# Three changes of order in a two-layer, two-block transformer kernel: third latent tile's weights, norm of x, first chunks of the next ada sums

## The chip, the cores and the metric

The kernel runs on one core of one Trainium2 chip. The metric is the device time of one execution in microseconds, as the median of several runs. The engines are TensorE (PE, matrix products), VectorE (DVE), ScalarE (ACT), GpSimd (POOL) and the queue of SyncE (SP), which issues most of the transfers. Each runs its own instructions in the order in which they are written, and they wait for each other by semaphores.

## The reference

Two transformer blocks of two layers each work on the same x of 256 tokens by 1024 columns, in float32. The first block modulates x by sums made from a conditioning vector c (six rows "ada" of 1024 for each layer), and normalises after each residual. The second takes the x of the first, projects it by a w_in of 4128 columns and runs three kinds of attention, of which one has latents at the end of these columns. Cut to what matters here:

```python
c_act = silu(c)
for l in range(2):                                    # first block
    ada = c_act @ w_ada[l] + b_ada[l]                 # sh1, sc1, gt1, sh2, sc2, gt2
    u = x * (1.0 + sc1) + sh1
    y = mixer(u, ...w_in[l]...)                       # attention, convolution, gates
    x = layer_norm(ALPHA * x + (1.0 + gt1) * y, ln_mix_g[l], ln_mix_b[l])
    u = x * (1.0 + sc2) + sh2
    h = square(relu(u @ w_up[l])) @ w_down[l]         # w_up 1024 x 4096
    x = layer_norm(ALPHA * x + (1.0 + gt2) * h, ln_ffn_g[l], ln_ffn_b[l])
for l in range(2):                                    # second block
    h = rmsnorm(x, ln_mix_g[l])
    proj = h @ w_in[l]                                # 1024 x 4128
    ...                                               # three attentions, gates, w_o, gated FFN
return rmsnorm(x, final_norm_g)
```

## The kernel before, in words

**Weights.** Every matrix of weights streams through a ring of four slots (class Weights, L91 to L190). A group is two chunks of 128 rows: 128 partitions by 2 x 512 numbers (2 x 344 for w_in of the second block, where a group comes as two transfers). SP asks for a group once the slot's last low part is made (L117 to L121); ACT makes the high part, a rounded copy (L128), after the landing and after PE has used the slot's last group; DVE makes the low part, raw less high (L134); PE multiplies three times for each chunk and each of the two token tiles: high by high, low by high, high by low (L148 to L150). Four groups make a tile of 512 (or 344) columns, 48 matmuls. So all engines go through the same list of groups, each in its own hand-written order of work between them.

**The first block's FFN.** Up-tile f is followed by down-tile f - 1 in the list of groups; T_FF is 8. DVE makes for each step f four low parts of down-tile f - 1, then in `hidden` (L1077) the squares of h, four low parts of up-tile f + 1, a row of the sum for gate 2 (`gate2_chunk`), chunk updates of the next layer's first ada sums (`next_chunk`, L1062: two instructions on 1024 columns, rows of w_ada times a number of c_act added to `ada_first`), and the low parts of the turned h (`aT`). In step 0 these are chunks 0 and 1, in step f chunk f + 1. SP issues the two fills of a chunk (`next_first`) ahead of the requests for an up-tile; they wait until the chunk two before is used.

**The start of layer 1.** DVE adds the last residuals, makes the rows of u for both token tiles with low parts of the first tile's weights between, then norms x itself for both token tiles (`normed`, two instructions of 1024 columns for each), which releases POOL's four loads for the convolution. After these come the low parts of the next weights, in a loop of four tiles, each with a row of the sum for gate 1 (L880) behind it.

**The start of the second block.** Four tiles of w_in, the latent columns, come first, into different banks of PSUM; the first is scaled by x_rstd on ACT (`take_scaled`) when it leaves its bank, and the fourth needs that bank. x_rstd is the root that POOL makes (`x_root`) from squares that ACT makes of the normed x (`square_x`). The norm of x (`last_x`) stands on DVE between the low parts of the second tile. At its end `first_left` is raised. POOL waits for that, issues a gather of 1.5 MB for the bias tables, and then makes the roots. SP too waits for it, having asked for two tiles of weights; it issues ten small loads of tables, then asks for the third tile.

## Time and profile before

| | us |
|---|---|
| median of 3 runs | 1920.86 (1920.22 to 1922.59) |
| the profiled execution | 1923.12 |
| its span in the profile | 1921.2 |
| PE busy, share of the span | 1807.1, 94% |
| DVE busy | 1310.8, 68% |
| ACT busy | 871.5, 45% |
| mean granted TensorE clock | 0.979 |

Times in the rows are microseconds from the span's start. In a timeline a row has the start, the duration, the engine, the line of the kernel, the operation, the tile it writes and those it reads, and the shapes; xN stands for N instructions merged into one row. A number in brackets is the idle time of the engine just before, with what ended it. Matmuls overlap, so their pace is read from their starts and not from their durations. SPq is SyncE's queue.

### The profile page before, as it was taken

How to read it: one execution, taken by the hardware profiler on the slowest of the kernel's cores; microseconds unless marked ns; L12 is line 12 of the kernel's file. 1: busy time of each engine (PE TensorE's matmuls, PEld its weight loads, DVE VectorE, ACT ScalarE, POOL GpSimd, SP SyncE). 2: the span in 40 equal slices, each digit the busy share in tenths (PEclk: the TensorE clock that was granted, in tenths of full speed). 3: DMA queues.
4: the chain of work that ended last, by engine and by line, in shares of the span. 5: the costliest groups of instructions: out<-in, count | busy, mean ns of one | idle time of the engine just before them, and what ended most of it. 6: DMA issues, size and time to landing. Idle time of an engine off the chain costs nothing.

```text
span 1921.2 us, 26005 instructions
## 1 busy us (share of the span) xinstructions
PE 1807.1 (94%) x8358; PEld 1423.2 (74%) x8358; DVE 1310.8 (68%) x2025; ACT 871.5 (45%) x1460; POOL 53.0 (3%) x112
## 2 busy tenths in 40 slices
PE   7989999998989999999699999999999999999998
PEld 3755777886765678887698777788879976778886
DVE  4679887667778986557455788655555478875555
ACT  1434434443434334443355565444445466644443
POOL 0000000000000000000000000000000000000000
PEclk9999999999999999998899999999999999999999
DMA  8755567773755547663456433465556653345554
GB/s 294 251 158 171 178 206 249 244 249 118 258 165 176 171 166 236 204 200 112 158 164 225 131 121 121 154 195 174 179 165 186 207 162 122 103 154 186 185 173 134
DMA packets 211186, 345.94 MB, mean 180 GB/s; under 512 B 20153, under 2 KB 95847, under 8 KB 210837
## 3 DMA queue, kind: packets, MB, share of 16 engines
q1 hardware_dynamic: 208774, 337.27, 54.4%
q0 software_dynamic: 2032, 6.97, 1.1%
q8 instruction: 53, 0.87, 0.2%
q10 hardware_dynamic: 288, 0.52, 0.1%
q14 instruction: 39, 0.32, 0.1%
HBM read 343.62 MB, written 1.07 MB: 179 GB/s over the span
## 4 chain that ended last, share of the span: by engine, by line
issue 52%; PE 30%; DVE 10%; DVEq 4%; ACT 1%; POOLq 1%; DMA 1%; SPq 1%; POOL 0%; ACTq 0%
PE prod L148 5%; PE prod L150 5%; PE prod L149 5%; PE acc L148 4%; PE acc L150 4%; PE acc L149 4%; DVE w_lo L134 3%; DVE conv_acc L917 2%; DVEq L916 2%; PE acc L1244 2%; PE turn L213 1%; DMA ada_rest<-in_w_ada_dram 1%; DVEq L775 1%; DVE stats L765 0%; DVE x_res L1013 0%
## 5 line engine op out<-in xcount | busy, mean ns | idle before, releaser
L134 DVE TENSOR_TENSOR w_lo<-w_raw,w_hi 128x1024 fp32r<-128x1024 f32 (+3 forms) x568 | 642.1, 1150 | 339.1 <-ACT w_hi L128 334.5
L128 ACT CAST w_hi<-w_raw 128x1024 fp32r<-128x1024 f32 (+3 forms) x568 | 554.2, 990 | 416.4 <-PE acc L150 197.0
L148 PE MATMUL prod<-w_hi,hT_hi 128*128 128x512 f32 (+1 forms) x880 | 332.2, 378 | 8.2 <-ACT kv_up L1687 1.8
L150 PE MATMUL prod<-w_hi,hT_lo 128*128 128x512 f32 (+1 forms) x880 | 323.9, 368 | 0.0
L149 PE MATMUL prod<-w_lo,hT_hi 128*128 128x512 f32 (+1 forms) x880 | 322.8, 367 | 0.0
L148 PE MATMUL prod<-w_hi,uT_hi 128*128 128x512 f32 x592 | 244.7, 413 | 17.1 <-DVE w_lo L134 8.0
L150 PE MATMUL prod<-w_hi,uT_lo 128*128 128x512 f32 x592 | 237.9, 402 | 0.0
L149 PE MATMUL prod<-w_lo,uT_hi 128*128 128x512 f32 x592 | 237.7, 402 | 0.0
L148 PEld LDWEIGHTS prod<-w_hi,hT_hi 128*128 128x128 f32 x880 | 166.4, 189 | 39.9 <-issue 7.3
L150 PEld LDWEIGHTS prod<-w_hi,hT_lo 128*128 128x128 f32 x880 | 166.6, 189 | 24.0
L149 PEld LDWEIGHTS prod<-w_lo,hT_hi 128*128 128x128 f32 x880 | 167.1, 190 | 21.2
L148 PEld LDWEIGHTS prod<-w_hi,uT_hi 128*128 128x128 f32 x592 | 113.4, 192 | 56.2 <-issue 17.4
L150 PEld LDWEIGHTS prod<-w_hi,uT_lo 128*128 128x128 f32 x592 | 113.6, 192 | 27.8
L149 PEld LDWEIGHTS prod<-w_lo,uT_hi 128*128 128x128 f32 x592 | 113.8, 192 | 24.5
L148 PE MATMUL acc<-w_hi,aT_hi 128*128 128x512 f32 x272 | 109.6, 403 | 7.3 <-DVE w_lo L134 4.5
L917 DVE SCALAR_TENSOR_TENSOR conv_acc<-hpad,conv_wT,conv_acc 128x256 f32<-128x256 f32 x232 | 102.5, 481 | 10.5 <-issue 1.3
L150 PE MATMUL acc<-w_hi,aT_lo 128*128 128x512 f32 x272 | 108.8, 400 | 0.0
L149 PE MATMUL acc<-w_lo,aT_hi 128*128 128x512 f32 x272 | 108.7, 400 | 0.0
L148 PE MATMUL acc<-w_hi,hT_hi 128*128 128x512 f32 (+1 forms) x144 | 57.2, 397 | 19.8 <-DVE w_lo L134 17.7
L148 PEld LDWEIGHTS acc<-w_hi,aT_hi 128*128 128x128 f32 x272 | 51.9, 191 | 22.0 <-issue 5.2
L1244 PE MATMUL acc<-ada_raw,c_wide 128*128 128x512 f32 x128 | 62.2, 632 | 0.0
L149 PEld LDWEIGHTS acc<-w_lo,aT_hi 128*128 128x128 f32 x272 | 51.9, 191 | 12.7 <-issue 0.2
(318 smaller groups left out, 2396.1 us busy)
## 6 DMA issues: line engine op xcount, KB each, us to landing
w_raw<-in_w_in_dram SPq DMA_DIRECT2D x72, 512.0 KB, 4.4
w_raw<-in_w_in_dram SPq DMA_DIRECT2D x192, 172.0 KB, 2.3
w_raw<-in_w_up_dram SPq DMA_DIRECT2D x64, 512.0 KB, 4.7
w_raw<-in_w_down_dram SPq DMA_DIRECT2D x64, 512.0 KB, 4.5
ada_raw<-in_w_ada_dram SPq DMA_DIRECT2D x52, 512.0 KB, 6.7
w_raw<-in_w_gate_dram SPq DMA_DIRECT2D x96, 256.0 KB, 3.2
w_raw<-in_w_ffn_gate_dram SPq DMA_DIRECT2D x88, 256.0 KB, 3.4
w_raw<-in_w_ffn_up_dram SPq DMA_DIRECT2D x88, 256.0 KB, 4.2
```

The costliest lines, as they stand in the source:

```text
L128: act.copy(self.hi[:, s, 0:cols], self.raw[:, s, 0:cols]).then_inc(self.hi_done, 1)
L134: dve.tensor_tensor(self.lo[:, s, 0:cols], self.raw[:, s, 0:cols], self.hi[:, s, 0:cols].bitcast(F32), ALU.subtract).then_inc(self.lo_done, 1)
L148: pe.matmul(out, a_hi, w_hi, start=first and c == 0, stop=False)
L149: pe.matmul(out, a_hi, w_lo, start=False, stop=False)
L150: mm = pe.matmul(out, a_lo, w_hi, start=False, stop=last and c == chunks - 1)
L213: t = pe.transpose(self.bank[b][0:rows, cols], src, self.ident)
L775: dve.drain()
L916: dve.drain()
L917: dve.scalar_tensor_tensor(out, rows, w, out, ALU.mult, ALU.add)
L1244: mm = pe.matmul(acc[0][:, :], c_wide[:, 2 * i + k, :], ada_raw[:, i, k * NT:(k + 1) * NT], start=i + k == 0, stop=False)
```

## The change

Three places are reordered.

- In layer 0's FFN, chunks 0 and 1 of the next layer's ada sums leave `hidden` of step 0. In step 1, chunk 0 stands behind the first two low parts of down-tile 0 and chunk 1 behind the other two. A drain follows chunk 1 too.
- At the start of layer 1, the norm of x of each token tile stands behind the first and the second low part of the loop, not ahead of all.
- At the start of the second block, SP asks for the third latent tile (groups 8 to 11) ahead of its wait for `first_left` and of the table loads. On DVE three low parts (6, 7, 8) stand between the norms of the two token tiles instead of two, and 9 to 11 behind `first_left`; on ACT the high parts 8 to 11 stand around the squares of x instead of behind them.

```diff
@@ first block, DVE, start of a layer
                     take_u_lo(3)
-                    for tok in range(TOKS):
-                        dve.drain()
-                        normed(x_res[:, tok, :], x_res[:, tok, :], tok, ln_vec[:, 0, :], ln_vec[:, 1, :]).then_inc(x_ready, 1)
...
                     for i in range(4):
                         W.split_lo(dve, Pos(4 + i, (l, G1), (t, 4)))
 
+                        if l > 0 and t == 0 and i < TOKS:
+                            dve.drain()
+                            normed(x_res[:, i, :], x_res[:, i, :], i, ln_vec[:, 0, :], ln_vec[:, 1, :]).then_inc(x_ready, 1)
@@ first block, DVE, next_chunk and hidden
                     if k == DC - 1:
                         dve.drain().then_inc(next_done, 1)
-                    elif k == 0:
+                    elif k < 2:
                         dve.drain()
...
                     if l < LAYERS - 1:
-                        for k in ((0, 1) if f == 0 else (f + 1,) if f < T_FF - 1 else ()):
-                            next_chunk(k)
+                        if 0 < f < T_FF - 1:
+                            next_chunk(f + 1)
...
                 for f in range(1, T_FF):
-                    split(Pos(at, (l, G1), (f, 8)))
+                    for g in range(0, 4, 2):
+                        split(Pos(at + g, (l, G1), (f, 8)), 2)
+                        if f == 1 and l < LAYERS - 1:
+                            next_chunk(g // 2)
@@ second block, SP
-                for t in range(2):
+                for t in range(3):
                     in_tile(IN2_T - LAT_TILES + t, layer(l, 4 * t, G2))
                 if l == 0:
                     sp.wait_ge(first_left, 1)
...
-                with sp.Fori(2, LAT_TILES) as t:
-                    in_tile(t + (IN2_T - LAT_TILES), Pos(0, (l, G2), (t, 4)))
+                for t in range(3, LAT_TILES):
+                    in_tile(IN2_T - LAT_TILES + t, layer(l, 4 * t, G2))
@@ second block, ACT
-                for tok in range(TOKS):
-                    square_x(2 * l, tok)
                 if l == 0:
-                    split(layer(l, 8, G2), 4, KG * IN2_W)
+                    split(layer(l, 8, G2), 1, KG * IN2_W)
+                    square_x(2 * l, 0)
+                    split(layer(l, 9, G2), 2, KG * IN2_W)
+                    square_x(2 * l, 1)
+                    split(layer(l, 11, G2), 1, KG * IN2_W)
+                else:
+                    for tok in range(TOKS):
+                        square_x(2 * l, tok)
@@ second block, DVE
-                    for tok in range(TOKS):
-                        split(layer(l, 4 + 2 * tok, G2), 2, KG * IN2_W)
-                        last_x(tok).then_inc(x_halves, 2)
+                    split(layer(l, 4, G2), 2, KG * IN2_W)
+                    last_x(0).then_inc(x_halves, 2)
+                    split(layer(l, 6, G2), 3, KG * IN2_W)
+                    last_x(1).then_inc(x_halves, 2)
                     dve.drain().then_inc(first_left, 1)
+                    split(layer(l, 9, G2), 3, KG * IN2_W)
...
-                with dve.Fori(1 if l == 0 else 0, LAT_TILES) as t:
+                with dve.Fori(2 if l == 0 else 0, LAT_TILES) as t:
                     split(Pos(4, (l, G2), (t, 4)), 4, KG * IN2_W)
```

## Rows read from the trace of the kernel before

**Rows 1.** Busy time by stretch: stretch, length, busy us, granted clock, DMA share, GB/s.

```profile
920.00:940.00 20.00, 5.46 (x35) 5.18 (x33) 4.44 (x6) 3.65 (x10) 3.61 (x11) 0.73 0.55 186
```

**Rows 2.** Waits of PE, whole span: who for whom, us in total, times, longest.

```profile
PE acc L148 <- DVE w_lo L134: 22.2, 6, 15.2
```

**Rows 3.** Timeline of DVE, layer 0's FFN, between steps 0 and 1.

```profile
291.48 5.05 DVE L1070 SCALAR_TENSOR_TENSOR ada_first<-ada_raw,c_act,ada_first 128x1024 f32<-128x1024 f32 x4
296.45 1.28 DVE L241 SCALAR_TENSOR_TENSOR aT_lo<-turn,aT_hi 128x512 fp32r<-128x512 f32 x2
297.82 4.63 DVE L134 TENSOR_TENSOR w_lo<-w_raw,w_hi 128x1024 fp32r<-128x1024 f32 x4
```

**Rows 4.** Timeline of PE there: first matmul of down-tile 0, first of up-tile 2.

```profile
299.19 0.76 PE L148 MATMUL acc<-w_hi,aT_hi 128*128 128x512 f32 x1 [4.51 <-DVE w_lo L134]
...
312.96 0.39 PE L148 MATMUL prod<-w_hi,uT_hi 128*128 128x512 f32 x1
```

**Rows 5.** Busy time behind that hole: PE, PEld, DVE, ACT, POOL, then granted clock.

```profile
299.20:304.40 5.20, 5.20 (x12) 4.09 (x13) 4.46 (x5) 0.00 (x0) 0.00 (x0) 0.50 0.78 246
```

**Rows 6.** Timeline of ACT there: the four high parts of down-tile 0.

```profile
289.63 2.00 ACT L128 CAST w_hi<-w_raw 128x1024 fp32r<-128x1024 f32 x2
...
295.21 1.04 ACT L128 CAST w_hi<-w_raw 128x1024 fp32r<-128x1024 f32 x1
```

**Rows 7.** DMA issues of the page: count, KB each, median us from issue to landing.

```profile
w_raw<-in_w_up_dram SPq DMA_DIRECT2D x64, 512.0 KB, 4.7
```

**Rows 8.** Timeline of DVE at the start of layer 1, norm of x and after.

```profile
489.66 1.28 DVE L774 SCALAR_TENSOR_TENSOR x_res<-x_res,mv,ln_vec 128x1024 f32<-128x1024 f32 x1
...
494.96 1.22 DVE L134 TENSOR_TENSOR w_lo<-w_raw,w_hi 128x1024 fp32r<-128x1024 f32 x1
496.27 0.75 DVE L880 SCALAR_TENSOR_TENSOR proj<-ada_raw,c_act,ada_b 128x512 f32<-128x512 f32 x1
```

**Rows 9.** Timeline of PE there: first matmuls of the second and the third tile.

```profile
496.23 0.80 PE L148 MATMUL prod<-w_hi,uT_hi 128*128 128x512 f32 x1 [3.54 <-DVE w_lo L134]
...
509.97 0.49 PE L148 MATMUL prod<-w_hi,uT_hi 128*128 128x512 f32 x1 [0.92 <-ACT proj L626]
```

**Rows 10.** Timeline of ACT there: high part of the third tile's third group.

```profile
508.29 1.05 ACT L128 CAST w_hi<-w_raw 128x1024 fp32r<-128x1024 f32 x1 [0.98 <-DMA w_raw<-in_w_in_dram]
```

**Rows 11.** Timeline of SP's queue: the request for that group.

```profile
500.12 0.37 SPq L121 DMA_DIRECT2D w_raw<-in_w_in_dram  x1
```

**Rows 12.** Timeline of SP's queue, second block: requests for weights from the third tile on.

```profile
930.37 29.12 SPq L121 DMA_DIRECT2D w_raw<-in_w_in_dram  x30
```

**Rows 13.** Timeline of ACT there: third tile's high parts, then the first tile's banks emptied.

```profile
938.93 1.62 ACT L128 CAST w_hi<-w_raw 128x688 fp32r<-128x688 f32 x2 [13.22 <-DMA w_raw<-in_w_in_dram]
...
942.23 0.98 ACT L1693 ACTIVATE proj_b<-prod,x_rstd 128x344 f32<-128x344 f32 x2
```

**Rows 14.** Timeline of POOL there: first operation behind the gather, last of the roots.

```profile
935.56 0.19 POOL L1644 TENSOR_TENSOR x_squares<-x_squares,small 128x1 f32<-128x1 f32 x1 [9.56 <-issue]
...
938.40 0.19 POOL L1658 TENSOR_TENSOR x_rstd<-x_rstd 128x1 f32<-128x1 f32 x1
```

**Rows 15.** Timeline of DVE there: low parts of the second tile, around the first norm.

```profile
915.63 1.66 DVE L134 TENSOR_TENSOR w_lo<-w_raw,w_hi 128x688 fp32r<-128x688 f32 x2
...
919.95 1.66 DVE L134 TENSOR_TENSOR w_lo<-w_raw,w_hi 128x688 fp32r<-128x688 f32 x2
```

**Rows 16.** Timeline of PE there: third tile, fourth tile, and what follows it.

```profile
940.66 0.65 PE L148 MATMUL acc<-w_hi,hT_hi 128*128 128x344 f32 x1 [15.20 <-DVE w_lo L134]
...
950.87 0.32 PE L148 MATMUL prod<-w_hi,hT_hi 128*128 128x344 f32 x1
...
958.44 3.61 PE L2286 MATMUL acc<-gates,proj_b 128*128 128x256 f32 x16
```

**Rows 17.** Timeline of POOL: power beside weight low parts (480.46), and with DVE idle.

```profile
480.46 1.34 POOL L591 TENSOR_TENSOR rstd<-var_eps,small 128x1 f32<-128x1 f32 x1
...
937.57 0.55 POOL L1646 TENSOR_TENSOR x_rstd<-x_squares,small 128x1 f32<-128x1 f32 x1
```

## Prediction, made before the changed kernel was run

> **What bounds the kernel now.** I read the table of 20 us stretches over the whole span first. PE is busy 94% of the time and most stretches of the feed-forward parts show it at 20.00 of 20. So only the holes can be bought, and I looked for the holes beside the three edited places. The deepest of the whole run is one of them: PE is busy 5.46 of 20 us at 920 to 940 [rows 1]. Next, what PE waited for: the low parts of weights, for the accumulating products 22.2 us in six waits, the longest 15.2 [rows 2]. Last, the timelines of every engine around each hole. They show three holes, all ended by a low part on DVE: 4.51 us before 299.19 [rows 4], 3.54 before 496.23 [rows 9], 15.20 before 940.66 [rows 16]. Each has a second price: PE comes back at the lower clock. Right behind the first hole the granted clock is 0.50 (1.2 GHz) and 12 matmuls fill 5.20 us [rows 5]. The reader should see in each timeline what DVE, or the queue, did just before the low part that PE missed; that is what the change moves.
>
> **Part 1, layer 0's FFN.** PE ends up-tile 1 at 294.68 (299.19 less 4.51) [rows 4]. DVE then still has the sum row of gate 2 to 291.5, four chunk updates of 1.26 us (291.48 to 296.5) and two aT low parts (to 297.7), and only at 297.82 the four low parts of down-tile 0 [rows 3]. The change takes the four chunk updates out. The aT low parts start at 291.5 and end at 292.8, then come weight low parts 1 and 2 at 1.16 each, done 294.1 and 295.3. Their high parts are there at 291.6 [rows 6]. Chunk 0 (2 x 1.26) runs to 297.8, low parts 3 and 4 end at 299.0 and 300.2 (the last high part is there at 296.3 [rows 6]), chunk 1 to 302.7. The drain added behind chunk 1 costs about 0.1 us, by the gap of 0.1 between the aT parts and the weight parts [rows 3].
> PE wants group 1 at 294.7, and it is ready at 294.1. Before, the tile took from 299.19 to 312.96, 13.77 us, of which the first 12 matmuls took 5.2 at the lower clock and the other 36 took 8.5, 0.236 each [rows 4, 5]. All 48 at 0.236 are 11.3 us. A group is a quarter, 2.8 us, so groups 2 to 4 are wanted at 297.5, 300.3 and 303.2, all behind their low parts. The tile ends at 306.0: a gain of 7.0 (4.5 of hole, 2.5 of clock).
> What is late next: up-tile 2. On SP its four requests stand behind the two fills of chunk 2, which wait for chunk 0. They go out at about 296.5 and 297.8, and the tile's first request at 298.3, still earlier than before. The median landing of such 512 KB is 4.7 us [rows 7], so 303.0; high part 1.05 and low part 1.2 [rows 6, 3] give 305.3, against 306.0 wanted. DVE is free for it at 304.1 (chunk 1 to 302.7, then two squares of h). The cover is 0.7 us; if two 512 KB fills ahead make it land after 8.1 us, the slowest such landing I use below, PE waits to 308.7 and the gain is 4.3. In step 1 DVE has three chunks: 8 low parts 9.6, six chunk updates 7.6, gate 2, squares and aT parts 1.3 each, 21.1 in all against a PE step of 22.7. Chunks 2 onward stand where they stood. I take 7.0, bounds 4.3 and 7.1.
>
> **Part 2, start of layer 1.** DVE spends 489.66 to 494.96 on the two norms of x, four instructions of 1.28 and drains [rows 8]; PE, free at 492.69, gets its low part at 496.2 [rows 9]. After: low part 1 from 489.9 to 491.1; norm of token tile 0 (2.65) to 493.8; an ada row of 0.75 [rows 8], to 494.6; low part 2 to 495.8; norm 1 to 498.5; row, 499.2; low part 3 to 500.4; row 501.2; low part 4 to 502.4. PE starts group 1 at 492.95 (ACT empties its bank), wants group 2 at 495.8 (ready at 495.9), group 3 at 498.7 (ready at 500.5: a new wait of 1.8), and ends the tile at 506.1. Before it ended at 509.05 (509.97 less 0.92 of waiting for ACT) [rows 9]. The next tile starts when ACT empties the bank, behind the high part at 508.29, whose weights were asked for at 500.12 and landed after 8.1 us [rows 10, 11]. That request now goes out at 500.5, 0.4 later, but the two ahead of it go out 5.0 and 2.4 earlier, into a DMA that was idle, so I let it land at about 505.7, an estimate between 4.7 us and 8.1 us after its request. PE restarts at 507.4 against 509.97: a gain of 2.5. Bounds: with 8.1 us again it restarts at 510.5, a loss of 0.6; with no new hole and no lower clock, 3.5 and 1.2 make 4.7. The lower clock after a hole of 1.8 us would cost at most what 6 matmuls at 0.43 cost over 0.236, 1.2. POOL's four loads behind the norm go out 3.5 us later; PE wants them 30 us on. That hides them.
>
> **Part 3, start of the second block.** The queue waits for the end of both norms, then issues ten table DMAs, and asks for tile 2's weights at 930.37 [rows 12]; ACT sees them at 938.93 [rows 13]. Now they are asked for as the slots come free: low parts of tile 1 run to 917.3 and 921.6 [rows 15], so groups 1 and 2 are asked for at 916.6 and 917.5, groups 3 and 4 at 920.9 and 921.8. DVE has group 1's low part at 922.5, norm 1 to 925.2, low parts 2 to 4 at 926.1, 927.0 and 928.5 (the last waits for ACT's square and high part). PE, free at 925.46, runs the tile at once and at the full clock: 950.87 to 958.44 for 48 matmuls of that width is 7.6 us [rows 16], so to about 933.0. Even with the worst landing here, 8.6 us for groups 3 and 4, it would end near 936.
> What is late next decides the gain. ACT must wait for x_rstd before it empties tile 0's bank and before it splits tile 3's weights, and x_rstd comes from POOL, behind POOL's gather: a DMA of 1.5 MB after which POOL stands 9.56 us, giving the root at 938.59 [rows 14]. The gather waits for the end of norm 1, which now stands behind one more low part, 0.87. So the root comes at 939.5. ACT then empties two banks (0.98 [rows 13]) and makes the high part at 940.5; before, PE started 1.73 after the start of such a high part (938.93 to 940.66 [rows 13, 16]), so tile 3 starts at 942.2 after a hole of 9.2 us. Its weights, asked for at 931.3 behind the tables (5.9 us of issuing, as before), land by 939.9 if they take the same 8.6. Tile 3 starts at the lower clock, as tile 2 did, and takes its 10.2 [rows 16]: end 952.4 against 958.4. A gain of 6.0: the tile of 7.6 goes into the hole, the root comes 0.9 later, the rest is rounding and latency. Bounds: if clock and root cost nothing more, 9.5; if the low parts beside the gather hold POOL for their whole 2.6 us, 3.4.
> What the rows say of that last point: POOL's power takes 0.55 us with DVE idle and 1.34 beside two weight low parts [rows 17], so POOL can be held by just these instructions, and three of them now run at 925 to 928.5, where DVE was idle. The Trainium skill (SBUF — State Buffer, Who interferes with whom) says that a tensor-tensor operation with both inputs in SBUF contends with what GpSimd reads, and infers that the writing of descriptors is not held by it. By that the sum would stay 6.0, by the row it could be 3.4.
>
> **Sum.** 7.0 + 2.5 + 6.0 = 15.5 us. Behind each place the trace is PE-bound or its other engines hang on PE, so the gains go through. The profiled execution took 1923.12 (span 1921.2), so 1907.6; the median of the runs is 2.26 lower, so 1905.4.
>
> **Rivals.**
> A: POOL is held by the low parts during the gather. For: [rows 17]. Against: the standing is 9.56 us with DVE idle, so it is work of its own kind. Part 3 gives 3.4: 1908.0. Chance 0.12.
> B: part 2 gives nothing. The DMA is full there, and the third request, now 0.4 later, lands after 8.1 us again [rows 10, 11]: 1908.5. Chance 0.12.
> C: part 3 gives more, because the 9.56 us shrink or the clock stays up: 3 us more, 1902. Chance 0.08.
> D: a later stage gives the time back. Layer 1's attention, where DVE is nearly full, or the tables that now come with tile 3's weights, would have to be the bound by their own time and not by PE's. Within 4 us of before, about 1919. Chance 0.03.
> E, slower: the FFN becomes paced by chunks. The fills of chunk k+2 stand on SP ahead of up-weights and wait for chunk k. If the weights then come later than PE wants them, each of the six further steps gets a hole of two chunk updates (2.5) and the clock's 2.3, 28.8 in all less 15.5: 1934. It decides from the point where the first landing of up-tile 2 is more than 0.7 us late and the lateness is handed on. Against: chunks from 2 on are not moved, and in later steps a chunk is used long before its slot's fill. Chance 0.03.
> F: the change does not do what it says: a first low part still late (part 1 at 4.3 or less), the rest as forecast: 1908.1. Chance 0.07.
> The forecast itself: 0.55.
>
> **Range and chances.** The bounds summed are 4.3 - 0.6 + 3.4 = 7.1 and 7.1 + 4.7 + 9.5 = 21.3, 1913.8 and 1899.6. All at one end is unlikely; 1901 to 1912 holds the forecast, A, B, C and F. A measurement tells about 0.2%, 3.8 us, from no change. All cases but D and E are faster by more: 0.94; D gives the same, 0.03; E slower, 0.03.
>
> **What would show it.** PE without a hole before down-tile 0, its clock not falling there, and up-tile 2 starting 11.3 us later. In layer 1 the 3.5 us hole gone and one of about 1.8 before the third group. In the second block a shorter hole, about 9 us, now before tile 3, ended by ACT behind x_rstd, and POOL still standing about 9.6 behind its gather; 12 would be rival A. Wrong would be: a hole before up-tile 2, ACT waiting over 7 us for the third weights of layer 1's tile 2, or holes in every FFN step.

## Result of the change, and the profile after

The changed kernel takes 1909.47 us (median of 5 runs, 1909.39 to 1912.9) against 1920.86 for the kernel before on the same chip (5 runs): a ratio of 0.9946, 95% interval 0.9934 to 0.9957. That is 11.4 us faster where 15.5 were forecast. The time lies inside the range of the prediction, 4.1 us above its forecast, and one of the three parts makes the kernel slower.

The profiled execution took 1909.42, its span is 1907.5. In the whole-span list of what PE waited for, the first line of before [rows 2] is down to 2.5 us. "prod" behind a low part has grown from 9.2 to 18.2 us, because the longest wait now stands there, and "ACT proj" from 0.9 to 5.6:

```profile
PE prod L148 <- DVE w_lo L134: 18.2, 12, 9.1
...
PE prod L148 <- ACT proj L626: 5.6, 3, 5.0
```

To see where the time went, I took both traces and compared the start of the same PE matmul, counted from the first one (8358 in both). The difference before and behind each edited place is what that place gave. This is worked out from the two traces, not a row of them. It is shown for all kernels in one table further down. For the changed kernel: part 1 -5.65 us, part 2 +2.64, part 3 -6.08, and -4.6 in places that no part touches.

**Place 1, layer 0's FFN.** Timeline of PE: the first matmul of down-tile 0 (against [rows 4]), then the first of up-tile 2. Behind it the timelines of ACT and of SP's queue: ACT's first high part of up-tile 2, and the requests.

```profile
294.25 0.39 PE L148 MATMUL acc<-w_hi,aT_hi 128*128 128x512 f32 x1
...
306.97 0.47 PE L148 MATMUL prod<-w_hi,uT_hi 128*128 128x512 f32 x1 [1.31 <-DVE w_lo L134]
```

```profile
304.51 1.05 ACT L128 CAST w_hi<-w_raw 128x1024 fp32r<-128x1024 f32 x1 [8.52 <-DMA w_raw<-in_w_up_dram]
```

```profile
296.16 1.54 SPq L473 DMA_DIRECT2D ada_raw<-in_w_ada_dram  x2
297.74 2.57 SPq L121 DMA_DIRECT2D w_raw<-in_w_up_dram  x4
```

The hole of 4.51 us is gone, each matmul starts 0.235 us after the last, and a new hole of 1.31 stands ahead of up-tile 2. It is ended by a low part of DVE. DVE waited there for ACT, and ACT for the DMA.

**Place 2, start of layer 1.** The timelines of DVE (against [rows 8]), PE (against [rows 9]), ACT (against [rows 10]), POOL and SP's queue (against [rows 11]).

```profile
485.61 1.28 DVE L774 SCALAR_TENSOR_TENSOR x_res<-x_res,mv,ln_vec 128x1024 f32<-128x1024 f32 x1
486.97 1.28 DVE L776 SCALAR_TENSOR_TENSOR x_res<-x_res,rstd,ln_vec 128x1024 f32<-128x1024 f32 x1
488.35 0.75 DVE L880 SCALAR_TENSOR_TENSOR proj<-ada_raw,c_act,ada_b 128x512 f32<-128x512 f32 x1
489.02 1.22 DVE L134 TENSOR_TENSOR w_lo<-w_raw,w_hi 128x1024 fp32r<-128x1024 f32 x1
```

```profile
494.83 0.50 PE L148 MATMUL prod<-w_hi,uT_hi 128*128 128x512 f32 x1 [1.45 <-DVE w_lo L134]
...
505.70 0.79 PE L148 MATMUL prod<-w_hi,uT_hi 128*128 128x512 f32 x1 [5.00 <-ACT proj L626]
```

```profile
504.03 1.04 ACT L128 CAST w_hi<-w_raw 128x1024 fp32r<-128x1024 f32 x1 [7.96 <-DMA w_raw<-in_w_in_dram]
504.98 1.08 ACT L626 ACTIVATE proj<-prod 128x512 f32 x2
```

```profile
493.58 0.58 POOL L598 DMA_DIRECT2D proj<-in_conv_dw_w_dram  x1 [17.35 <-DVE x_res L776]
494.16 0.51 POOL L599 DMA_DIRECT2D proj<-in_conv_dw_b_dram  x1
494.66 0.58 POOL L601 DMA_DIRECT2D ln_vec<-in_conv_ln_g_dram  x1
495.23 0.55 POOL L601 DMA_DIRECT2D ln_vec<-in_conv_ln_b_dram  x1
```

```profile
494.94 0.37 SPq L121 DMA_DIRECT2D w_raw<-in_w_in_dram  x1
```

The hole of 3.54 us became one of 1.45, as meant. Then PE stands 5.00 us where it stood 0.92. Its releaser is ACT's emptying of a bank, but that stands in ACT's order behind a high part whose weights were asked for at 494.94 and came at 504.03: 9.1 us. POOL's four loads were issued from 1.4 us ahead of that request to 0.3 us behind it.

**Place 3, second block.** Tiles 2 and 3 are the third and the fourth latent tile; as in the prediction they are counted from 0. Timelines of PE (against [rows 16]), POOL (against [rows 14]) and ACT (against [rows 13]).

```profile
936.41 0.62 PE L148 MATMUL prod<-w_hi,hT_hi 128*128 128x344 f32 x1 [9.07 <-DVE w_lo L134]
```

```profile
919.77 1.09 POOL L1642 DMA_DIRECT2D gates<-bias_rows_dram  x1 [17.12 <-DVEq L1993]
...
930.66 0.19 POOL L1647 TENSOR_TENSOR x_squares<-x_squares,small 128x1 f32<-128x1 f32 x1 [9.39 <-issue]
...
933.49 0.19 POOL L1661 TENSOR_TENSOR x_rstd<-x_rstd 128x1 f32<-128x1 f32 x1
```

```profile
933.72 0.99 ACT L1696 ACTIVATE proj_b<-prod,x_rstd 128x344 f32<-128x344 f32 x2 [12.26 <-POOL x_rstd L1661]
```

Tile 2 now runs without a hole at 919.60. The hole is one tile later, ahead of tile 3, and 9.07 us long instead of 15.20. PE's low part there waited for ACT, and ACT for POOL's root.

### The profile page after: what moved, and what is told of

The parts are those of the page before. It is cut to its first block, busy times and chain, and to the rows that moved or that the text cites. A ratio compares the mean times of both kernels' runs of the same rounds, so it can differ in the third digit from the quotient of the medians.

```text
span 1907.5 us, 25910 instructions
## 1 busy us (share of the span) xinstructions
PE 1798.7 (94%) x8358; PEld 1414.7 (74%) x8358; DVE 1310.7 (69%) x2025; ACT 871.0 (46%) x1460; POOL 53.1 (3%) x112
## 4 chain that ended last, share of the span: by engine, by line
issue 52%; PE 28%; DVE 11%; DVEq 4%; DMA 2%; ACT 1%; POOLq 1%; SPq 1%; POOL 0%; ACTq 0%
PE prod L148 5%; PE prod L149 5%; PE prod L150 5%; PE acc L148 3%; PE acc L150 3%; PE acc L149 3%; DVE w_lo L134 3%; DVE conv_acc L917 2%; DVEq L916 2%; PE acc L1247 2%; PE turn L213 1%; DMA w_raw<-in_w_in_dram 1%; DMA ada_rest<-in_w_ada_dram 1%; DVEq L775 1%; DVE proj L776 1%
## 5 line engine op out<-in xcount | busy, mean ns | idle before, releaser
L150 PEld LDWEIGHTS acc<-w_hi,aT_lo 128*128 128x128 f32 x272 | 51.2, 188 | 12.5
```

The costliest lines, as they stand in the source:

```text
L150: mm = pe.matmul(out, a_lo, w_hi, start=False, stop=last and c == chunks - 1)
```

## Experiments

**One part at a time.** First the kernel before with part 1 alone.

```diff
-                    elif k == 0:
+                    elif k < 2:
                         dve.drain()
...
-                        for k in ((0, 1) if f == 0 else (f + 1,) if f < T_FF - 1 else ()):
-                            next_chunk(k)
+                        if 0 < f < T_FF - 1:
+                            next_chunk(f + 1)
...
-                    split(Pos(at, (l, G1), (f, 8)))
+                    for g in range(0, 4, 2):
+                        split(Pos(at + g, (l, G1), (f, 8)), 2)
+                        if f == 1 and l < LAYERS - 1:
+                            next_chunk(g // 2)
```

> Part 1 alone. Theory (each part acts by itself, as the two traces show it matmul by matmul): the 4.5 us hole before down-tile 0 is gone with its lower clock, and a hole of about 1.3 us stands before up-tile 2, so 5.7 us less than before, about 1915.2. Rival (the gain of part 1 is given back where layer 1 starts, and only the three together show it): within 2 us of before.

Measured: 1913.44 (5 runs) against 1919.95 (16 runs of the kernel before), ratio 0.9952 (0.9935 to 0.997). Here and below, the ratios with their intervals are not quotients of the two medians; that would be 0.9966 here, inside the interval. At place 1 PE gained 5.5 us, and a hole of 1.43 stands ahead of up-tile 2. Part 1 is worth what it gave in the changed kernel.

Then part 2 alone: the kernel before with only the norm of x between the low parts.

```diff
-                    for tok in range(TOKS):
-                        dve.drain()
-                        normed(x_res[:, tok, :], x_res[:, tok, :], tok, ln_vec[:, 0, :], ln_vec[:, 1, :]).then_inc(x_ready, 1)
...
+                        if l > 0 and t == 0 and i < TOKS:
+                            dve.drain()
+                            normed(x_res[:, i, :], x_res[:, i, :], i, ln_vec[:, 0, :], ln_vec[:, 1, :]).then_inc(x_ready, 1)
```

> Part 2 alone. Theory: PE gains 3 us on the second tile of layer 1 and then waits about 5 us for ACT, whose third high part waits for weights that land 9 us after their request; with the lower clock behind that hole part 2 loses 2.3 us, about 1923.2. Rival (as I forecast: the long landing is chance or comes from the shift that part 1 makes, and part 2 by itself gains): 2.5 us less, 1918.4, with ACT waiting under 3 us for these weights.

Measured: 1923.61 (10 runs, 1921.22 to 1927.28) against 1919.95 (16 runs of the kernel before), ratio 1.0017 (1.0007 to 1.0028). Alone, the part makes the kernel slower. Timeline of PE, the same matmul as in [rows 9], with the same new wait:

```profile
511.55 0.79 PE L148 MATMUL prod<-w_hi,uT_hi 128*128 128x512 f32 x1 [4.46 <-ACT proj L626]
```

The loss at the place is 3.25 us. So the loss needs no other part of the change.

Part 3 alone (the changed kernel without parts 1 and 2; against the kernel before, with the edits on ACT cut here):

```diff
-                for t in range(2):
+                for t in range(3):
                     in_tile(IN2_T - LAT_TILES + t, layer(l, 4 * t, G2))
...
-                    for tok in range(TOKS):
-                        split(layer(l, 4 + 2 * tok, G2), 2, KG * IN2_W)
-                        last_x(tok).then_inc(x_halves, 2)
+                    split(layer(l, 4, G2), 2, KG * IN2_W)
+                    last_x(0).then_inc(x_halves, 2)
+                    split(layer(l, 6, G2), 3, KG * IN2_W)
+                    last_x(1).then_inc(x_halves, 2)
                     dve.drain().then_inc(first_left, 1)
+                    split(layer(l, 9, G2), 3, KG * IN2_W)
```

> Part 3 alone. Theory: tile 2 runs without a hole, PE stands about 9 us before tile 3, ended by ACT behind x_rstd, and POOL stands 9.4 to 9.6 us behind its gather though three low parts run beside it; 6.0 us less, 1914.9. Rival (the 6 us came partly from a lucky clock phase of 1.8 us in this stage): between 4 and 8 us less, with the hole the same.

Measured: 1913.62 (6 runs), ratio 0.9962 (0.9949 to 0.9975). The place gave 6.8 us by the traces, the hole ahead of tile 3 is 9.01 us, and POOL stood 9.34 us behind its gather, beside three low parts of DVE.

Parts 1 and 3 together, the norm of x back in its old place (the second diff above, undone in the changed kernel):

> Parts 1 and 3, part 2 undone. Theory: 2.3 us faster than the changed kernel, about 1907.2, with the 3.5 us hole back in layer 1 and no 5 us wait for ACT. Rival (part 2 gains 2.5 and something else in the changed kernel lost 4): about 1912.

Measured: 1905.63 (4 runs, 1903.31 to 1907.14), ratio 0.9915 (0.9895 to 0.9934). It is 3.8 us below the changed kernel, by medians from two chips. By medians against the kernel before, part 1 alone gave -6.5, part 2 +3.7, part 3 -6.3, together -9.2 before rounding, and the changed kernel -11.4. Each interval reaches some 2 to 3.5 us to either side, so within them the parts add.

**What makes part 2 slower.** The changed kernel, in which POOL may issue its four loads only after the second tile's rows:

```diff
-                            normed(x_res[:, i, :], x_res[:, i, :], i, ln_vec[:, 0, :], ln_vec[:, 1, :]).then_inc(x_ready, 1)
+                            normed(x_res[:, i, :], x_res[:, i, :], i, ln_vec[:, 0, :], ln_vec[:, 1, :])
...
+                    if l > 0 and t == 1:
+                        dve.drain().then_inc(x_ready, TOKS)
                 dve.drain().then_inc(gate1_done, 1)
```

> The changed kernel, but POOL's four loads of layer 1 are released after the second tile's rows (some 15 us later) and not at the end of the norm. Theory (the loads slow the requests for weights that now stand right behind them: in the changed kernel the third high part of tile 2 waits 9.0 us for its landing): it lands in about 5 us, PE waits under 1.5 us for ACT there and keeps its clock, 4 to 5.4 us faster than the changed kernel, about 1904.5. Rival (SP's own fills and weights fill the DMA): the landing stays above 8 us and the time within 1 us of the changed kernel.

Measured: 1904.74 (4 runs), ratio 0.9918 (0.99 to 0.9936). Timelines of SP's queue and ACT: the request that took 9.1 us in the changed kernel.

```profile
494.07 0.37 SPq L121 DMA_DIRECT2D w_raw<-in_w_in_dram  x1
```

```profile
498.66 1.05 ACT L128 CAST w_hi<-w_raw 128x1024 fp32r<-128x1024 f32 x1 [3.69 <-DMA w_raw<-in_w_in_dram]
```

It lands after 4.6 us, and PE waits 0.50 us where it waited 5.00. The late loads stand at 505.66 to 507.32 here. A request of 512 KB beside them lands late too, after 7.7 us, but PE has no wait near it. The two rows of busy time that follow are of the changed kernel and of this one, over the same stretch of work (columns: stretch, its length, busy us of PE, PEld, DVE, ACT and POOL, granted clock, DMA share, GB/s):

```profile
494.00:501.00 7.00, 5.87 (x24) 4.44 (x24) 6.82 (x8) 1.06 (x1) 1.78 (x4) 1.00 0.64 182
```

```profile
493.00:500.00 7.00, 5.88 (x24) 4.44 (x24) 6.82 (x8) 2.39 (x3) 0.00 (x0) 1.00 0.71 220
```

With POOL's loads under way, less is moved in all, not only less of SP's. Counted over the 7 us from the request on, it is 217 GB/s against 260.

Which of the four loads does it? Two are small (62 and 2 KB), two are rows broadcast to 128 partitions (256 KB each). In the next kernel the two small ones go out as in the changed kernel and the broadcasts late; in the one after, the broadcasts go at once and the small ones late:

```diff
                 pool.dma_start(conv_rows[0:CONV_K, :], dr["conv_dw_w"][ls].rearrange("a k c -> (a k) c")).then_inc(vec_in, 16)
                 pool.dma_start(conv_rows[CONV_K:CONV_K + 1, :], dr["conv_dw_b"][ls, :]).then_inc(vec_in, 16)
+                if l > 0:
+                    pool.wait_ge(x_late, l)
                 for n, name in enumerate(("conv_ln_g", "conv_ln_b")):
                     pool.dma_start(cln_vec[:, n, :], dr[name][ls, :].to_broadcast([P, CW])).then_inc(vec_in, 16)
...
+                    if l > 0 and t == 1:
+                        dve.drain().then_inc(x_late, 1)
```

> The changed kernel; in layer 1 GpSimd lets only its two small loads (the convolution's rows, 62 and 2 KB) go behind the norm of x, and its two broadcast loads (256 KB each in SBUF) go after the second tile's rows. Theory: it is the bytes and packets of the two broadcasts that hold up the weights asked for at 494.94 in the changed kernel. Then the third group lands 4.6 to 5.2 us after its request, PE waits 0.4 to 1 us near 500 us where it waited 5.00, and the time is that of the kernel with all four loads late, 1904.7 (1903 to 1906.5). Rival: any load on GpSimd's queue that is under way slows SP's, small or not: PE waits 3 us or more and the time is 1907.5 to 1909.5.

> The changed kernel; in layer 1 GpSimd's two broadcast loads go at once behind the norm of x, and its two small loads after the second tile's rows. Theory: the broadcasts carry the harm, so that this kernel is like the changed one: the third group lands 8 to 9 us after its request, PE waits 4 to 5 us near 500 us, 1909.5 (1907.5 to 1911). The broadcasts now go out 1.1 us earlier, since the two small issues of 0.58 and 0.51 us no longer stand ahead; that can take up to 1.1 us off the wait. Rival (small loads carry it): PE waits under 1 us, 1904.7.

Measured: broadcasts late 1904.12 (4 runs), broadcasts at once 1907.61 (4 runs). PE's wait at the place, small loads early first, broadcasts early second:

```profile
501.05 0.49 PE L148 MATMUL prod<-w_hi,uT_hi 128*128 128x512 f32 x1 [0.26 <-ACT proj L629]
```

```profile
502.99 0.49 PE L148 MATMUL prod<-w_hi,uT_hi 128*128 128x512 f32 x1 [2.96 <-ACT proj L629]
```

The small loads are harmless: 495.01 to 499.37 is 4.4 us. The broadcasts carry it: 494.27 to 501.32 is 7.1 us. That is less than the 8 to 9 us I expected. Here the broadcasts were issued at 492.91 and 493.50, both ahead of the request; in the changed kernel at 494.66 and 495.23, around it. How near they stand does not settle the landing by itself: in the kernel before, the request stands 3.4 us behind the first broadcast and still lands after 8.1 us. The loss of rate is small here too, 253 GB/s over the 7 us from the request on. Why this order costs less stays open.

Is the norm's new place worth anything, once the loads are late? The norm back at its old place, the loads late:

> The changed kernel with the norm of x of layer 1 back at its old place ahead of the low parts, and GpSimd's loads let go late, after the second tile's rows. Theory: the two halves of part 2 are separate: moving the norm between the low parts removes the 3.5 us wait of PE before group 3, and the earlier loads cost what they cost. Then this kernel has the wait of about 3.5 us back before group 3, no 5 us wait near 500 us, and stands 2 to 3 us above the kernel with the moved norm and late loads (1904.7): 1907 to 1908, against 1905.6 for the kernel with the old norm and the loads where they were. Rival: the norm's place is worth nothing once the loads are late, because the third group's weights or the next request then end last instead: the time is that of the moved norm with late loads within 1 us (1904 to 1905.7), and PE's offset against it is the same behind the stage.

Measured: 1907.53 (5 runs, 1904.99 to 1911.76), 2.8 us above the kernel with the moved norm and late loads. The traces say 2.2 at the place (-0.99 against -3.20), with PE's hole back; timeline of PE:

```profile
489.56 0.50 PE L148 MATMUL prod<-w_hi,uT_hi 128*128 128x512 f32 x1 [3.52 <-DVE w_lo L134]
```

The theory holds. This kernel also says something of the kernel before. There the requests of this stage at 496.36, 498.32 and 500.12 landed after 4.3, 7.8 and 8.1 us. The same three, with the norm in the same place and the loads late, landed after 3.4, 4.8 and 5.6 us. So part of the 8.1 us of before was already the work of these loads, but PE lost only 0.92 us by it [rows 9]. What I can't settle is the worth of late loads with the norm at its old place: the traces give 0.9 us to it, the medians (1907.53 against 1905.63, on other chips) give the opposite.

**Part 1, the last hole.** The changed kernel, with up-tile 2's weights requested ahead of chunk 2's fills:

```diff
-                    if l < LAYERS - 1:
+                    if l < LAYERS - 1 and f != 1:
                         next_first(f + 1)
                     up(f + 1, Pos(at + 4, (l, G1), (f, 8)))
+                    if l < LAYERS - 1 and f == 1:
+                        next_first(f + 1)
```

> The changed kernel, but SP asks for up-tile 2's weights ahead of the two fills of chunk 2. Theory (the two fills of 512 KB in front make the first high part wait): the hole of 1.3 us before up-tile 2 is gone, 1.3 us faster, about 1908.2. Rival (DVE is what is late, with its third chunk in this step): the hole stays above 1 us, or moves behind up-tile 2 because chunk 2 comes late.

Measured: 1909.68 (4 runs), ratio 0.9941 (0.9922 to 0.996), no different from the changed kernel. The trace shows the mechanism all the same; timelines of SP's queue and of ACT's first high part of up-tile 2:

```profile
295.40 6.35 SPq L121 DMA_DIRECT2D w_raw<-in_w_up_dram  x4
```

```profile
300.31 1.05 ACT L128 CAST w_hi<-w_raw 128x1024 fp32r<-128x1024 f32 x1 [2.75 <-DMA w_raw<-in_w_up_dram]
```

The first request goes out 2.3 us earlier and lands after 4.9 us instead of 6.8. There is no hole ahead of the tile, the rival (DVE is late) did not happen, and the place gave 7.19 us instead of 5.65. The median does not show the 1.5 us (1909.68 against 1909.47). In the profiled execution, PE came to the place 1.6 us later than in the changed kernel's, through work that the edit doesn't touch.

**Part 3, what holds tile 3.** The changed kernel with POOL's gather behind the roots, so that x_rstd no longer waits for it:

```diff
-            pool.wait_ge(first_left, 1)
-            pool.wait_ge(bias_rows.in_dram, 16)
-            pool.dma_start(bias_flipped, bass.AP(tensor=scratch.tensor, offset=0,
-                                                 ap=[[1, P], [REL, AH + BH], [1, SEQ]])).then_inc(bias_in, 16)
+            def gather():
+                pool.wait_ge(first_left, 1)
+                pool.wait_ge(bias_rows.in_dram, 16)
+                pool.dma_start(bias_flipped, bass.AP(tensor=scratch.tensor, offset=0,
+                                                     ap=[[1, P], [REL, AH + BH], [1, SEQ]])).then_inc(bias_in, 16)
...
             for l in range(LAYERS):
                 x_root(2 * l)
+                if l == 0:
+                    gather()
```

> The changed kernel, but POOL makes the roots of the first x ahead of its gather. Theory (the gather's 9.4 us held ACT, and the weights of tile 3 stand ready just behind it): ACT empties tile 0's bank about 10 us earlier, but PE still stands until the weights of tile 3 land, asked for at 926.3 behind the tables; they land no earlier than before, so the hole stays 8 to 11 us and the time within 3 us of the changed kernel. Rival (the root alone is the bound): the hole shrinks to under 3 us, 8 us faster.

Measured: 1910.82 (4 runs), ratio 0.9946 (0.9928 to 0.9964): nothing gained. Timeline of ACT:

```profile
923.12 0.99 ACT L1699 ACTIVATE proj_b<-prod,x_rstd 128x344 f32<-128x344 f32 x2 [2.15 <-POOL x_rstd L1662]
934.55 0.76 ACT L128 CAST w_hi<-w_raw 128x688 fp32r<-128x688 f32 x1 [10.44 <-DMA w_raw<-in_w_in_dram]
```

ACT has the root 10 us earlier and then waits for tile 3's weights until the same time. Behind the root stood a second limit at the same place: the request for tile 3, behind the tables on SP's queue. So both have to go. The next kernel also asks for that tile ahead of the tables:

```diff
-                for t in range(3):
+                for t in range(4):
                     in_tile(IN2_T - LAT_TILES + t, layer(l, 4 * t, G2))
```

> As the run before, and SP asks for the fourth latent tile too ahead of first_left and the tables. Theory (two things end at the same point, the root and the weights, and both must go): no hole before tile 3 and no lower clock, with at most 2 us of waiting before the bias products for the gather or the tables; 9 to 11.5 us faster than the changed kernel, about 1899. Rival (the gather and the tables then end last): a hole of 5 us or more before the bias products, 6 us faster or less.

Measured: 1904.99 (4 runs), ratio 0.9913 (0.9894 to 0.9932), 5.8 us below the last kernel. By the traces the place gave 12.84 us instead of 5.78. As expected, there is no hole ahead of tile 3 and none before the bias products. But I expected 9 to 11.5 us against the changed kernel, and it is 4.5 by the medians and 6.8 at the place. What I had left out is the tile behind the latent ones, whose weights are still asked for behind the tables. ACT waits for them, and PE for ACT; timelines of PE and ACT:

```profile
945.76 0.42 PE L148 MATMUL prod<-w_hi,hT_hi 128*128 128x344 f32 x1 [3.34 <-ACT proj_b L1697]
```


```profile
942.81 2.46 ACT L128 CAST w_hi<-w_raw 128x688 fp32r<-128x688 f32 x3 [8.79 <-DMA w_raw<-in_w_in_dram]
```

**All four edits together** (late loads, up-tile 2 ahead of the fills, roots ahead of the gather, four tiles ahead of the tables):

> The changed kernel with the four edits of the runs before together: GpSimd's four vector loads of layer 1 let go after the second tile's rows, up-tile 2 asked for ahead of chunk 2's fills, GpSimd's roots ahead of the table gather, and the fourth latent tile asked for ahead of the tables. If the four act in different places and add, the sum is made from medians of the runs so far: the changed kernel 1909.5, less 4.7 for the loads (1904.7 against 1909.5), less 4.5 for the root with the fourth tile (1905.0 against 1909.5), less 1.7 for the request ahead of the fills (by its trace alone): 1898.5, within 1896 to 1901. In the trace: no wait of PE above 1 us near 500 us, none before up-tile 2, none before latent tile 3. Rival: the places share something later (the gather and the tables end last in the latent stage whatever comes before), so that time saved ahead of it is given back there: 1902 to 1905, with PE's wait for ACT at the fourth latent tile grown beyond the 3.34 us of the run with roots first and the fourth tile ahead.

Measured: 1895.94 (4 runs, 1893.98 to 1897.05) against 1919.78, ratio 0.9872 (0.9857 to 0.9888). It beats both kernels, the changed one by 13.5 us. The sum of the single gains was 11, for a forecast of 1898.5 (1896 to 1901); the traces give 1.5, 5.9 and 6.4 at the three places, 13.8. The edits add, and the rival (time given back in the latent stage) did not happen. Of the holes that the change had left or made, two stay: 1.46 us ahead of the third group at the start of layer 1, and PE's wait at the tile behind the latent ones. Timeline of PE at the former place of the 5.00 us wait and at that tile:

```profile
499.13 0.49 PE L148 MATMUL prod<-w_hi,uT_hi 128*128 128x512 f32 x1 [0.43 <-ACT proj L628]
...
934.75 0.65 PE L148 MATMUL prod<-w_hi,hT_hi 128*128 128x344 f32 x1 [3.80 <-ACT proj_b L1701]
```

**The places side by side.** Microseconds that PE lost (+) or gained (-) at each place against the kernel before, by the start of the same matmul; "elsewhere" is what the rest of the kernel gave. All but the medians come from one profiled execution each.

| kernel | FFN | layer 1 | second block | elsewhere | median |
|---|---|---|---|---|---|
| changed | -5.65 | +2.64 | -6.08 | -4.6 | 1909.47 |
| part 1 alone | -5.52 | -0.19 | -0.95 | -1.1 | 1913.44 |
| part 2 alone | 0 | +3.25 | -1.06 | -3.5 | 1923.61 |
| part 3 alone | -0.09 | -0.06 | -6.84 | -5.0 | 1913.62 |
| parts 1 and 3 | -5.49 | -0.10 | -5.73 | -4.6 | 1905.63 |
| late loads | -5.58 | -3.20 | -7.00 | -4.3 | 1904.74 |
| small loads early | -6.34 | -3.43 | -5.83 | -3.2 | 1904.12 |
| broadcasts early | -5.78 | -0.73 | -5.83 | -5.1 | 1907.61 |
| old norm, late loads | -5.78 | -0.99 | -5.77 | -5.5 | 1907.53 |
| up-tile 2 ahead | -7.19 | +3.71 | -7.51 | -3.0 | 1909.68 |
| roots first | -5.27 | +2.86 | -5.78 | -3.8 | 1910.82 |
| roots and fourth tile | -5.30 | +3.78 | -12.84 | -3.2 | 1904.99 |
| all four | -7.19 | -3.27 | -12.44 | -5.3 | 1895.94 |

The same order of work still gives different numbers from kernel to kernel: 5.3 to 6.3 us in the FFN, +2.6 to +3.8 in layer 1, 5.7 to 7.5 in the second block. So differences of up to 1 us in the first two columns, and of up to 2 us in the third, say nothing. "Elsewhere" is 3 to 5.5 us in every kernel but one, even in the slower one, so most of it seems to belong to the one execution of the kernel before that all are held against; it was itself 2.3 us above its median. The medians agree with that. Held against the median of the kernel before from the same chip, eleven of the thirteen kernels lie within 1.6 us of what their three places give; the changed kernel (2.3) and parts 1 and 3 together (3.0) are faster than their places.

## Why the prediction was right, and where not

**Part 1, forecast 7.0, measured 5.65.** The mechanism was right to the step: no hole ahead of down-tile 0, no fall of the clock, both chunks hidden. The failed term is the cover of 0.7 us ahead of up-tile 2. I let its weights land 4.7 us after the request, at 303.0. They were asked for at 297.74 and landed at 304.5, 6.8 us later, behind two fills of 512 KB issued 1.6 us ahead. I had that case (8.1 us, 4.3 gained) as the bound, and 5.65 lies between. The kernel with these requests first gained 7.19, so this was all that was missing from the 7.0. In it the requests also go out earlier, so it does not part the two; with 4.7 us from 297.74 the low part would have been ready at about 304.7, ahead of PE (305.66), by the prediction's own sum.

**Part 2, forecast 2.5, measured -2.64, outside its bounds of 4.7 and -0.6.** (The lower bound has a slip: 500.5, 8.1 and 1.68 make 510.3, a loss of 0.3.) Every step up to the third request was right: the new hole is 1.45 us (1.8 forecast), the request goes out 0.4 us later against the work around it. The step that failed is the last sentence: "POOL's four loads behind the norm go out 3.5 us later; PE wants them 30 us on. That hides them." It asked only who waits for the loads, not whom they hold up. Timeline of POOL in the kernel before, the two broadcasts:

```profile
496.73 0.58 POOL L601 DMA_DIRECT2D ln_vec<-in_conv_ln_g_dram  x1
497.30 0.55 POOL L601 DMA_DIRECT2D ln_vec<-in_conv_ln_b_dram  x1
```

They stood 3.4 and 2.8 us ahead of the critical request at 500.12 [rows 11]. After, they stand at 494.66 and 495.23, around the request at 494.94, because the norm that releases them moved less than the requests did. The request lands after 9.1 us, where I took 5.2 and had 8.1 as the worst: 3.9 of the 5.1 us missing. The runs with late loads and with late broadcasts put it at 4.6 and 4.4 us. The rest is the clock, for which the lower bound had no term: PE came back from the hole of 5.00 at the lower level (1.2 GHz), and its offset grew by 1.3 us from there on. Busy time behind the hole, the granted clock is the 0.52:

```profile
505.70:508.80 3.10, 3.10 (x8) 2.48 (x9) 3.01 (x4) 1.33 (x2) 0.00 (x0) 0.52 0.94 328
```

Rival B came nearer, with no gain for that part and a total of 1908.5, and had half of the reason. The landing was late again, but the DMA was not simply full: 182 GB/s over the stretch, against 220 without the loads. The 8.1 us of [rows 10, 11], which rival B took for a full DMA and I for the slowest landing, was itself partly the work of these loads: it was 5.6 us in the kernel with the old norm and late loads.

**Part 3, forecast 6.0, measured 6.08.** The hole was forecast at 9.2 and is 9.07, between tiles 2 and 3, ended by the root, and POOL stood 9.39 us (9.56 before) with three low parts beside it. Rival A (12 us) is refuted by that row, and by the 9.01 to 10.13 us of the other kernels with the same order there. By the Trainium skill (SBUF — State Buffer, Who interferes with whom), the writing of descriptors is not held by a tensor-tensor operation on DVE, which the page gives as inferred; the trace does not speak against it, 9.39 us beside them and 9.56 without. It shows the whole standing and not the writing of descriptors by itself. What the part took as a given is why POOL stands. The DMA view has the gather's landing, here in the kernel before:

```profile
gates<-bias_rows_dram POOLq DMA_DIRECT2D x1, 1536.0 KB, 10.7
```

Issued at 924.69, it landed at 935.4, and POOL went on at 935.56 [rows 14]. In the changed kernel it is 919.77, 930.5 and 930.66. What the part left open: tile 3's weights were as late as the root, which I had worked out (939.9 against 940.5) but not named as a second limit. The kernel with roots first ran into it.

**The sum.** The three places gave 9.1 us by the traces where 15.5 were forecast: 1.4 too much in part 1, 5.1 in part 2. That the time is only 4.1 above the forecast is owed to 4.6 us in the pair of traces (2.3 in the medians) that I had put at zero. That is luck: with the three places alone it would have been 1911.8, just inside the range of 1901 to 1912. Part of the 4.6 us has a place. Two stretches that no part touches run at a higher granted clock after. Over 1512 to 1532 it is 0.91 before and 1.00 after; over 900 to 920 it is 0.74 before and 0.97 after:

```profile
900.00:920.00 20.00, 16.80 (x79) 15.30 (x80) 15.93 (x23) 5.28 (x9) 1.71 (x2) 0.74 0.18 54
```

```profile
900.00:920.00 20.00, 18.41 (x107) 16.31 (x107) 17.33 (x22) 8.64 (x16) 1.94 (x3) 0.97 0.42 125
```

These two rows hold work that is shifted by 5 to 6 us, so the clock is to be compared with care; by the start of the same matmul PE gained 1.5 us from 898 to 925 and 2.1 from 1512 to 1532. Why the clock was lower there in one and not in the other was not tried. Against the same execution of the kernel before, eleven of the thirteen kernels gain 1.0 to 1.5 us at the first and eleven 1.8 to 3.2 us at the second, the others nothing, edited nearby or not. So I count them to no edit, and most likely to that one execution. Rivals D and E did not happen: nothing was given back, and the later FFN steps have no holes.

## What to carry to other kernels

When an operation is moved, follow what it releases on other queues to whom it disturbs there, not only to who waits for it: a transfer that nobody needs for 30 us doubled the landing of the one that PE needed next. When a hole has a limit, work out which limit stands second and how close: here the root and the weights were within a microsecond, and only taking both away gave the time. A trace compared matmul by matmul can show a gain of 1.5 us that the medians did not. It takes several kernels to trust it: here the FFN gave 7.19 us in both kernels with the edit and 5.3 to 6.3 in the nine without.

## What the runs showed of the hardware

- Broadcast loads on GpSimd's queue (two of 256 KB) slow what SP's queue moves at the same time by more than their bytes: a request of 512 KB landed after 9.1 us instead of 4.6, while the whole core moved 182 GB/s instead of 220. Issued 1.4 us ahead of the request, they made it 7.1 us, at 253 GB/s over the 7 us from the request on (260 with late loads, 217 in the changed kernel). Two small loads on the same queue (62 and 2 KB) did nothing (4.4). The Trainium skill (DMA: Bandwidth & Descriptors, Issuing engines are not separate DMA queues) says that transfers of all issuing engines run interleaved on the same 16 DMA engines; the trace agrees in that the one landed later, and it shows a loss of total rate besides. Whether it is the broadcast or the queue that costs so much was not tried.
- In these traces POOL goes on behind its gather of 1.5 MB only when the gather has landed. In all eleven kernels with the gather ahead of the roots, it lands 10.3 to 11.4 us after its issue, and POOL's next operation but one, with a drain in front of it, starts 0.1 to 0.2 us after the landing, whether low parts of DVE run beside it or not. Its standing is 9.0 to 10.1 us. That is a reading of eleven traces; no kernel was made to test it.
- POOL's small operations are slow beside DVE's norm of x. With the roots first, its addition took 1.23 us and its power 1.58, each started 0.1 us behind an instruction of the norm (916.29 and 917.65). With DVE idle they take 0.19 and 0.56. Timeline of POOL:

```profile
916.40 1.23 POOL L1648 TENSOR_TENSOR x_squares<-x_squares,small 128x1 f32<-128x1 f32 x1
917.77 1.58 POOL L1650 TENSOR_TENSOR x_rstd<-x_squares,small 128x1 f32<-128x1 f32 x1
```
